# A hybrid decoder block with routed experts: the first step's row list on chip, one step per pass, regions moved

## The reference

```python
def moe(h, w_router, b_router, w_gate_up, b_gate_up, w_down, b_down):
    logits = (t @ w_router + b_router).astype(jnp.float32)      # 1024 x 32
    top_val, top_idx = lax.top_k(logits, TOP_K)                 # 4 of 32 experts per token
    gate = jax.nn.softmax(top_val, axis=-1)
    ...                                                         # (token, weight) sorted by expert, in chunks of 128 rows
    def expert_block(args):
        xc, e = args
        gu = xc @ w_gate_up[e] + b_gate_up[e]
        g, u = gu[:, :D_EXPERT], gu[:, D_EXPERT:]
        g = jnp.minimum(g, SWIGLU_LIMIT)
        u = jnp.clip(u, -SWIGLU_LIMIT, SWIGLU_LIMIT)
        act = (u + 1.0) * (g * jax.nn.sigmoid(SWIGLU_ALPHA * g))
        return act @ w_down[e] + b_down[e]
    ...                                                         # out[token] += weight * y
return rmsnorm(x + moe(...), norm_final_g)
```

## Time and profile before

| | us |
|---|---|
| median of 3 runs | 2152.6 (2151.63 to 2152.64) |
| the profiled execution | 2151.84 |
| its span, first to last instruction | 2150.2 |
| TensorE busy | 2004.9 (93%) |
| VectorE busy | 1598.8 (74%) |
| ScalarE busy | 1293.9 (60%) |
| GpSimd busy | 290.8 (14%) |
| mean granted TensorE clock | 0.973 |

### The profile page before, as it was taken

The page is one execution under the profiler, slowest core; times in us unless marked ns, Lnnn a source line. Parts: engine busy times, 40 slices in busy tenths (PEclk is TensorE's granted clock), DMA queues, the critical chain, the costliest instruction groups (busy, mean ns, idle before and its releaser), DMA issues.

```text
span 2150.2 us, 37083 instructions
## 1 busy us (share of the span) xinstructions
PE 2004.9 (93%) x11768; PEld 1532.1 (71%) x11769; DVE 1598.8 (74%) x2100; ACT 1293.9 (60%) x1755; POOL 290.8 (14%) x334
## 2 busy tenths in 40 slices
PE   6999899999898399999999999999999999999993
PEld 5777677777687277777777777777777777777772
DVE  4778755545655488797877779977878988977894
ACT  5555454444533267676665667766667767755774
POOL 3100000000124201111112111121101101210100
PEclk9999999999998699999999999999999999999996
DMA  5020111010634769798888889978889979878994
GB/s 175 20 98 1 40 40 40 20 39 1 215 133 140 170 219 378 279 341 313 286 291 291 283 290 380 375 264 286 287 290 377 376 260 375 311 258 285 377 339 165
DMA packets 256003, 489.57 MB, mean 228 GB/s; under 512 B 20043, under 2 KB 38311, under 8 KB 255856
## 3 DMA queue, kind: packets, MB, share of 16 engines
q1 hardware_dynamic: 233824, 439.56, 57.2%
q0 software_dynamic: 21088, 49.35, 8.7%
q10 hardware_dynamic: 1040, 0.00, 0.0%
HBM read 461.01 MB, written 32.05 MB: 229 GB/s over the span
## 4 chain that ended last, share of the span: by engine, by line
PE 80%; DVE 7%; issue 4%; ACT 4%; DMA 2%; SPq 1%; POOL 0%; ACTq 0%; DVEq 0%; POOLq 0%
PE psum L749 15%; PE psum L750 14%; PE psum L753 14%; PE psum L766 8%; PE psum L455 3%; PE psum L585 3%; PE psum L589 3%; PE psum L587 3%; PE psum L457 2%; PE psum L456 2%; PE psum L737 2%; PE psum L692 1%; PE psum L716 1%; DVE o_lo L1490 1%; PE psum L693 1%
## 5 line engine op out<-in xcount | busy, mean ns | idle before, releaser
L1679 DVE TENSOR_TENSOR w_lo<-ring,w_hi 128x1024 fp32r<-128x1024 f32 x768 | 914.9, 1221 | 142.8 <-ACT w_hi L1056 131.5
L1056 ACT ACTIVATE w_hi<-ring 128x1024 fp32r<-128x1024 f32 x768 | 803.6, 1059 | 275.1 <-PE psum L753 265.9
L749 PE MATMUL psum<-w_hi,rows_hi 128*128 128x512 f32 x1024 | 422.1, 412 | 4.2 <-DVE rows_lo L1683 2.5
L750 PE MATMUL psum<-w_hi,rows_lo 128*128 128x512 f32 x1024 | 399.9, 391 | 0.0
L753 PE MATMUL psum<-w_lo,rows_hi 128*128 128x512 f32 x1024 | 316.2, 390 | 0.0
L749 PEld LDWEIGHTS psum<-w_hi,rows_hi 128*128 128x128 f32 x1024 | 193.8, 189 | 46.7 <-issue 10.3
L753 PEld LDWEIGHTS psum<-w_lo,rows_hi 128*128 128x128 f32 x1024 | 192.5, 188 | 41.1
L750 PEld LDWEIGHTS psum<-w_hi,rows_lo 128*128 128x128 f32 x1024 | 193.2, 189 | 37.5
L749 PE MATMUL psum<-w_hi,act_hi 128*128 128x512 f32 x512 | 219.8, 429 | 0.0
L750 PE MATMUL psum<-w_hi,act_lo 128*128 128x512 f32 x512 | 202.8, 396 | 0.0
L766 PE MATMUL psum<-ring,region_m 128*32 128x256 f32 x3072 | 174.2, 380 | 0.0
(11 more groups left out here) (333 smaller groups left out, 2997.7 us busy)
## 6 DMA issues: line engine op xcount, KB each, us to landing
ring<-in_w_gate_up_dram SPq DMA_DIRECT2D x128, 2048.0 KB, 16.1
ring<-in_w_down_dram SPq DMA_DIRECT2D x64, 2048.0 KB, 14.1
ring<-in_w_in_dram SPq DMA_DIRECT2D x16, 512.0 KB, 5.2
region_m<-in_x_dram SPq DMA_DIRECT2D x8, 512.0 KB, 11.6
ring<-in_w_in_dram SPq DMA_DIRECT2D x2, 2048.0 KB, 17.5
ring<-in_w_out_dram SPq DMA_DIRECT2D x2, 2048.0 KB, 7.5
region_a<-in_x_dram POOLq DMA_DIRECT2D x8, 512.0 KB, 4.8
acc_rows<-region_a POOLq DMA_DIRECT2D x8, 512.0 KB, 3.3
```

Source lines behind the costliest of these rows:

```text
L749: mm(bank(i), hi[:, ks], wh, start=(k0 + q == 0), stop=False)
L750: mm(bank(i), lo[:, ks], wh, start=False, stop=False)
L1056: act.activation(w_hi[:, n % NBUF, :], place[i][:, k0 * HALF:(k0 + 2) * HALF], ACT.Copy).then_inc(hi_done, 1)
L1679: v.tensor_tensor(out=w_lo[:, n % NBUF, :], in0=place[i][:, k0 * HALF:(k0 + 2) * HALF], in1=w_hi[:, n % NBUF, :].bitcast(f32), op=ALU.subt ...
```

## The change

1. **The list of step 0 is made on chip.** Slots below 128 of expert 0 are step 0's rows. VectorE's new `first_rows(lo, hi)` makes, for each token, its smallest slot, the weight that belongs to a slot below 1024, and a row with a one at the slot (`first_hot`). TensorE multiplies `first_hot` with (token - 4096, weight), summed over the eight tiles, and VectorE writes the result into `meta`. Six tiles are done ahead of `top(7)`, the last two after `place_rows(7)`.
2. **GpSimd gathers step 0's rows** as soon as that is there, ahead of the scatters of tiles 6 and 7, and waits for the scatters after that. SyncE starts units 2 and 3 only after the gather has landed. TensorE transposes the rows first and the table's columns after them.
3. **TensorE's loop has one step per pass**, 64 passes. There is one buffer of rows and one selector. The other engines' loops stay.
4. **The regions lie in another order**: ring, `region_s`, `region_a`, `region_m`. `region_s` now starts at 147584, `region_a` at 163968, `region_m` at 190080, all multiples of 128.
5. **`entry` and `slot_i`** move from the ring to `region_s`, since the scatters are still to come when `w_lo` is written.

```diff
-        at_m = next_base()
-        region_m = sb("region_m", [P, LM * (SEQ + 3) + LM * SEQ])
         at_s = next_base()
         region_s = sb("region_s", [P, LM * SEQ])
         at_a = next_base()
         region_a = sb("region_a", [P, A_COLS])
+        at_m = next_base()
+        region_m = sb("region_m", [P, LM * (SEQ + 3) + LM * SEQ])
...
-        rows_g = [region_m[:, 0:D], region_m[:, 2 * D:3 * D]]
+        rows_g = region_m[:, 0:D]
...
@@ sync
-            for i in range(4):
+            for i in range(2):
+                unit(i, 0)
+            sp.wait_ge(rows_in, 16)
+            for i in range(2, 4):
                 unit(i, 0)
@@ tensor, in the loop over t, after rank(t - 3)
+                if t == NT + 1:
+                    pe.wait_ge(first_built, 1)
+                    for s in range(NT - 2):
+                        mm(bank(5)[:, 0:2], first_hot[:, s, :], first_row[:, s, :], start=(s == 0), stop=False)
             for s in range(NT):
                 last = mm(bank(1)[:, 0:NE], ones_b[:], mask_b[:, s, :], start=(s == 0), stop=(s == NT - 1))
             last.then_inc(count_mm, 1)
+            pe.wait_ge(first_built, 2)
+            for s in range(NT - 2, NT):
+                last = mm(bank(5)[:, 0:2], first_hot[:, s, :], first_row[:, s, :], start=False, stop=(s == NT - 1))
+            last.then_inc(count_mm, 1)
...
             pe.wait_ge(slot_done, NT)
-            pe.wait_ge(rows_in[0], 16)
-            rows_turn(0)
+            pe.wait_ge(rows_in, 16)
+            rows_turn()
+            pe.wait_ge(columns_done, 1)
+            for q in range(4):
+                last = tr(bank(0)[0:1, q * P:(q + 1) * P], tab_c[:, q:q + 1], ident[:])
+            last.then_inc(columns_mm, 1)
             pe.wait_ge(table_done, 1)
...
-            with pe.Fori(0, MAXS // 2) as pair:
-                for u in range(2):
-                    j = pair * 2 + u
-                    with pe.If(j < total):
+            with pe.Fori(0, MAXS) as j:
+                with pe.If(j < total):
@@ gpsimd
-            for t in range(NT - 3, NT):
-                scatter(t)
+            scatter(NT - 3)
             for q in range(2):
                 pool.wait_ge(acc_out[q], 16 * (NT // 2))
                 pool.wait_ge(h2_out[q], 16 * (NT // 2))
-            pool.wait_ge(scattered, 16 * NT * TOPK)
...
-            g.dma_start(meta[:, 0, :], chunks[0]).then_inc(meta_in, 16)
+            pool.wait_ge(first_meta, 1)
+            gather(0)
+            scatter(NT - 2)
+            scatter(NT - 1)
+            pool.wait_ge(scattered, 16 * NT * TOPK)
             for half in (slice(0, HALF), slice(HALF, 3 * QC), slice(3 * QC, D)):
                 ...
-            pool.wait_ge(meta_in, 16)
-            gather(0)
...
-                            wait_reg(pool, meta_in, j * 16 + 32)
+                            wait_reg(pool, meta_in, j * 16 + 16)
+                            wait_reg(pool, rowsT_mm, j + 1)
                             gather(1 - u)
@@ vector
+            def first_rows(lo, hi):
+                ts = slice(lo, hi)
+                n = hi - lo
+                v.tensor_reduce(out=first_at[:, ts], in_=slot_f[:, ts, :], axis=AX, op=ALU.min)
+                then(v.scalar_tensor_tensor(out=first_w[:, ts, :], in0=slot_f[:, ts, :], scalar=float(SEQ),
+                                            in1=entry[:, ts, :, 1].bitcast(f32), op0=ALU.is_lt, op1=ALU.mult))
+                v.tensor_reduce(out=first_row[:, ts, 1:2], in_=first_w[:, ts, :], axis=AX, op=ALU.add)
+                v.tensor_tensor(out=first_hot[:, ts, :], in0=bc(iota_s[:, None, :], [P, n, P]),
+                                in1=bc(first_at[:, ts, None], [P, n, P]), op=ALU.is_equal).then_inc(first_built, 1)
             top(NT - 2)
             place_rows(NT - 3)
+            v.tensor_scalar(first_row[:, :, 0], iota_t[:], iota_p, float(-FAR), ALU.add, ALU.add)
+            first_rows(0, NT - 2)
             top(NT - 1)
             place_rows(NT - 2)
             place_rows(NT - 1)
+            dve.wait_ge(slot_done, NT)
+            first_rows(NT - 2, NT)
+            dve.wait_ge(count_mm, 2)
+            v.tensor_scalar(meta[:, 0, 0:1], bank(5)[:, 0:1], float(FAR), None, ALU.add)
+            v.tensor_copy(meta[:, 0, 1:2].bitcast(f32), bank(5)[:, 1:2]).then_inc(first_meta, 1)
...
-                            if n == 4:
-                                selector(1 - u, e_next)
...
                             for n in range(NBUF):
                                 low(n, j + 1)
+                            wait_reg(dve, unit_mm[5], j + 1)
+                            wait_reg(dve, tdown_mm, before + tail + 1)
+                            selector(e_next)
```

More of the change, by code:

```diff
@@ L149, in hybrid_decoder_block @@
         actT_tail = region_m[:, 5376:5376 + 2 * P]
-        sel_cur = region_m[:, 7680:7680 + P].bitcast(bf16).rearrange("p (u s) -> p u s", u=2)
+        sel_cur = region_m[:, 7680:7680 + P // 2].bitcast(bf16)
         igate = unit_view(region_s[:, :], LM)
@@ L305, in hybrid_decoder_block @@
         unit_mm = [sem(f"unit_mm{i}") for i in range(NU)]
+        first_built, first_meta = sem("first_built"), sem("first_meta")
         rank_read, rowsT_mm, rowsT_done, meta_in, tmeta_in, add_at_done = (
             sem(n) for n in ("rank_read", "rowsT_mm", "rowsT_done", "meta_in", "tmeta_in", "add_at_done"))
-        rows_in, trows_in = [sem(f"rows_in{u}") for u in range(2)], sem("trows_in")
+        rows_in, trows_in = sem("rows_in"), sem("trows_in")
         hi_done, lo_done, sub_mm, rows_lo_done, act_lo_done = (
@@ L706, in _, with rows_turn @@
             last.then_inc(count_mm, 1)
[L708 to L714, removed]
+            pe.wait_ge(first_built, 2)
+            for s in range(NT - 2, NT):
+                last = mm(bank(5)[:, 0:2], first_hot[:, s, :], first_row[:, s, :], start=False, stop=(s == NT - 1))
+            last.then_inc(count_mm, 1)
+            def rows_turn():
                 for k in range(KD):
-                    last = tr(bank(6, 2)[:, k * P:(k + 1) * P], rows_g[u][:, k * P:(k + 1) * P], ident[:])
+                    last = tr(bank(6, 2)[:, k * P:(k + 1) * P], rows_g[:, k * P:(k + 1) * P], ident[:])
                 last.then_inc(rowsT_mm, 1)
@@ L1670, in _, with selector @@
             total = dve.value_load(ends[0:1, 0:1], min_val=1, max_val=MAXS)
-            def selector(u, e):
-                v.tensor_copy(sel_cur[0:96, u, :], eq[0:96, ds(e, 1)].to_broadcast([96, P])).then_inc(sel_ready, 1)
+            def selector(e):
+                v.tensor_copy(sel_cur[0:96, :], eq[0:96, ds(e, 1)].to_broadcast([96, P])).then_inc(sel_ready, 1)
             def low(n, j):
@@ L1684, in rows_low @@
                                 op=ALU.subtract).then_inc(rows_lo_done, 1)
-            selector(0, 0)
+            selector(0)
             dve.wait_ge(rowsT_done, 1)
```

164 lines of the change are left out of this document (85 added, 79 removed).

## The result

The changed kernel takes **2128.2 us** (median of 4 runs, 2127.9 to 2130.1) against 2152.6 of the kernel before: a ratio of 0.9888, 95% interval 0.9871 to 0.9905. Measured again in a later batch of runs the ratio was 0.9890 (0.9873 to 0.9906). The prediction was 2125, in a range of 2114 to 2142.

The account below looks back on a forecast made before the run. The prediction saw the loop bound by TensorE, and before it a hole waiting for step 0's rows. Handover -17.6, regions -8.1 and -2.5, one step per pass +1.2 make -27.0: from 2151.8 to 2125 us, range 2114 to 2142.

Parts of the forecast that it names:

- The row list and the gather's start: Handover: list made on chip, six tiles' 1.7 us hidden before top(7), gather issued at 700.0 us.
- The gather's landing: Handover: step 0's rows land at R = 709 us, behind scatters slowed by weights; bounds 704.4 and 714.4.
- Landing to first product: Handover: first expert product at R + 8.8 us, R being the rows' landing; the table is late next.
- Units 2 and 3: First expert's later weights: issued at 709.3 us, both in at 728, wanted at 727 and 732, hidden.
- The handover's sum: Part 1, from the row list to the first expert product: -17.6 us, ends -22.3 and -12.3.
- The regions: Expert loop: operands on multiples of 128 save 6 ns per product, 48 a step: -8.1 us, between 0 and -10.
- The prediction's doubt about m_lo: m_lo lies on a multiple of 128, yet its products take 401 ns: neighbours are slowed too, or something else.
- Ahead of the loop 2.1 of 2.5: Before the expert loop: regions' order saves 2 us in the output projection, 0.5 in o products: -2.5 us, between 0 and -5.
- One step per pass: TensorE's expert loop: six more tail steps followed by a pass start with a gap: +1.2 us, bounds -1 and +3.0.
- The fourth rival: TensorE's loop: stalls at each pass start make the kernel slower; 3 us a jump gives 2216 us. Chance 4%.
- gather unhindered: Handover: rows land at 704.4 us, free of earlier scatters; -22.3 us for part 1, total 2120. Chance 15%.
- the place isn't it: Expert loop and projection: regions' places don't cause the slower products; parts 1 and 3 alone, -16.4 us, 2135. Chance 15%.

Follow-up runs that it names:

- after_again: The changed kernel itself, unedited, run again in a later batch: 2127.3 us, ratio 0.9890 to the kernel before.
- hold_none: Changed kernel with weight units 2 and 3 issued without waiting for the gathered rows: 2132.9 us, ratio 0.9918 to the kernel before.
- columns_first: Changed kernel with TensorE's four transposes of the table columns put ahead of its wait for the rows: 2123.8 us, ratio 0.9876 to the kernel before.
- regions_only: Kernel before with only the order of the regions changed to the changed kernel's: 2144.1 us, ratio 0.9971 to the kernel before.
- no_regions: Changed kernel with the regions back in the order of the kernel before: 2134.4 us, ratio 0.9927 to the kernel before.
- two_steps: Changed kernel with two steps in each pass of TensorE's loop again: 2125.6 us, ratio 0.9888 to the kernel before.
- m_off64: Changed kernel with region_m (rows_hi, rows_lo) moved by 64 bytes: 2148.6 us, ratio 0.9990 to the kernel before.
- a_off32: Changed kernel with region_a (act_hi, act_lo) moved by 32 bytes: 2149.8 us, ratio 1.0002 to the kernel before.

## Why the prediction was right, step by step

**The row list and the gather's start: right.** The path from the last comparison went as laid out: 696.88, products 697.35, meta done at 698.63, gather at 699.54 (predicted 700.0). The first six tiles' 1.7 us were hidden before top(7), as said.

**The gather's landing: right in size, its cause not shown.** Predicted 709, measured 707.5. The prediction had the weights slow the scatters and the gather land 2 us behind the last of these. The weights' part is shown: with none in flight the gather takes 4.3 to 4.6 us instead of 7.9 to 9.0. That they act through the scatters ahead is not: after_again fits (1.7 us behind the last scatter), hold_none doesn't (5.1), and the loop's gathers take 7 to 8 us beside weights with no scatter near. So the right size is partly luck. The Trainium skill (DMA: Bandwidth & Descriptors, queues, rings and completion order) has the descriptors of one ring taken in order, and turns between queues packet by packet. It also says that a later descriptor may finish its write before an earlier one, so "can't pass" was more than it states. In the runs with both landings on record the gather landed behind the last scatter ahead of it, which agrees with the order. The turns alone don't explain its time: see the stretch of columns_first without a packet of the weights.

**Landing to first product: right.** R + 8.5 against R + 8.8, with table_done at R + 6.0 instead of 6.3. That the table is late next was the prediction's point; columns_first shows the 4 us directly.

**Units 2 and 3: right.** Issued at 707.95, the last landed at 728.02, wanted by ScalarE near 730.7. Predicted 728 and 732.

The handover's sum was -17.6; it measured 58.3 - 39.6 = 18.7 less. One caution: regions_only, with before's handover, took 54.7, so a single execution of it is good for 4 us either way.

**The regions: right in sign, mis-sized in the loop.** The term was -8.1, from 6 ns at each of 48 products. Groups of act_lo and w_lo did lose 5, but the third that I had not read, act_hi with w_hi, went from 429.4 to 426.7 only: (5.1 + 5.1 + 2.7) / 3 = 4.3 ns. The prediction's doubt about m_lo is answered as it supposed: those products fell from 401 to 395 ns though m_lo lay at a fast place before and after, so they had been slowed by their neighbours. 4.3 x 48 x 32 = 6.6 us, and the wait for VectorE at the first activation transposes grew from 0.73 to 0.80 us in some 16 steps, 1.1: 5.5, which is what no_regions measured (5.7); regions_only gave 3.7. From no_regions to the changed kernel a step with a tail became 0.22 us shorter, where 0.29 were forecast, and one without 0.10, where 0.22 were: there the wait for VectorE grew by 0.07 us, which is more than the 12 products that I had left out for it are worth at 4.3 ns. Ahead of the loop 2.1 of 2.5 came.

**One step per pass: right.** +1.2 predicted, 1.1 (two_steps) to 2.0 (no_regions) measured. The fourth rival, 3 us a pass, is refuted. By the Trainium skill (Runtime: NRT & Kernel Launch, instruction fetch mechanics) a taken branch beyond the loaded window would cost a fetch; the gaps of 0.13 to 0.18 us show none here, and no instruction packet ran from 860 us on.

**The rest.** Of the profiled execution's 21.8 us, -18.7 is handover, -2.1 output projection, -3.7 loop; +1.4 came before the output projection and +1.2 in the final norm. The first of these need not be the change's: over the changed kernel and its variants with the same early code the output projection began anywhere between 569.6 and 572.8 us. For this execution the forecast was 2124.8, so it came out 5.2 us over: 3.2 in the loop (2.6 of it the regions' term), 1.4 and 1.2 where nothing was forecast, 0.4 in the output projection, and 1.1 less in the handover. It is also the slowest of the four runs; their median is 3 us over the forecast. Of the rivals "gather unhindered" would have been right without unit 1 in flight (4.3 to 4.6 us), "the place isn't it" is refuted by no_regions and m_off64.

## What to carry to other kernels

When a small gather must land soon, count the bulk loads in flight before you count the small writes ahead of it. In the one execution of each that was profiled, holding one more 2 MB load back took the gather from 8.0 to 4.5 us, and holding the last one back too starved the step that the gather was for. When a wait is removed, look at once for what stood beside it for free: four tiny transposes moved behind the rows cost 4 us. And read every group that shares a cost before giving one price to all; a rule on addresses is to be tried at a second place before it is believed.

## What the runs showed of the hardware

- A 512-column product whose 128x128 stationary tile lies badly takes some 5 ns longer (395 against 390 ns listed). 96 such products in each of 32 steps add up to 15.9 us (m_off64), and 144 in each to 16.5 (a_off32). Off by 32 or by 64 bytes is the same. The 32-column tail products didn't react: 380 ns in every variant.
- A gather of 128 rows of 4 KB took 4.3 to 4.6 us at the handover without 2 MB loads in flight, 7.9 to 9.0 with one and 10.7 with three. In the loop, away from the scatters, it took 7.1 to 8.4 us beside loads at 310 to 330 GB/s and 4.3 to 5.4 without. Scatters of 128 entries of 16 bytes took 3 us without such loads and 10 beside them. By which way the loads do it isn't shown.
